# A mixture-of-experts step: spare quads moved to odd places, their up stage moved forward, selection before row broadcasts, last matrices in halves

## The chip, the cores and the metric

The kernel runs on one core of one Trainium2 chip. The metric is the device time of one execution in microseconds (us); the time before is the median of three runs. Five engines work side by side, each with its own in-order queue: TensorE (PE in the profile; its weight loads are PEld), VectorE (DVE), ScalarE (ACT), GpSimd (POOL) and SyncE (SP), which here only issues transfers (DMA) and waits. They meet at counters (semaphores): an instruction raises one when it ends, and another engine's queue stands still until the counter has reached a number.

## The reference, cut to what matters

Two layers, two streams of 128 tokens (256 tokens in all), width 1024. Each layer has a modulated norm, three mixers side by side with shared input and output projections, and then a mixture of 32 experts. The change touches only the experts:

```python
hid = silu(einsum('bnd,edf->bnef', h, moe_w1)) * einsum('bnd,edf->bnef', h, moe_w3)
return einsum('bnef,efd->bnd', hid * gate[..., None], moe_w2)
```

`gate` is not zero for two experts of one group per token, so there are 512 pairs of token and expert in a layer. Each expert has three matrices of 1 MiB in 32-bit floats: two up (1024x256) and one down (256x1024).

## The kernel before, in words

**Tiles and quads.** A tile holds up to 32 tokens of one expert; a quad is four tiles. Eight base quads hold one tile of each of the 32 experts, so their matrices are always loaded. Four spare quads hold 16 further tiles, for experts that more than 32 tokens chose. Which expert a spare tile belongs to is found at run time (`eid`, L1837 to L1840); SP reads it into a register, and the loads of a spare tile without tokens are issued under a condition that skips them. The list `ORDER` says which quad stands in which of the twelve places: before, 0, 1, 8, 2, 3, 9, 4, 5, 10, 6, 11, 7, where 8 to 11 are the spares. Two places in a row make a batch, whose 256 token slots are gathered together.

**A quad's weights.** A quad needs 12 matrices in three thirds of 4 MiB: `up_weights(i, 0)` for tiles 0 and 1 into four slots of `ring_b`, `up_weights(i, 1)` for tiles 2 and 3 into four slots of `ring`, `down_weights(i, 0)` and `(i, 1)` into the last two slots of each (L628 to L651). Each slot exists once, so a load into it waits until the product that reads it is done: the first third of place i+1 waits for the first up stage of place i (`up_psum`), the down third of place i+1 for the down stage of place i (`down_psum`). A spare quad passes through the same slots and waits, also when all its loads are skipped. SP issues, for each place i: both up thirds; then, if place i-1 was a spare, its down third; then, if i is no spare, its own down third (L665 to L675).

**A place on TensorE** (L1424 to L1451), in this order: `up(i)` if i is no spare (two stages of 64 products, for two tiles each, L1398); `gather` of a quarter of the next batch (L1380); `combine(i-1)`, which adds the result of the place before to the tokens (L1409); `gather` of another quarter; two transposes of the hidden values (L1437); if place i+1 is a spare, `up(i+1)`; then the two halves of the down product (L1449). ScalarE takes silu of the first up bank (`gated`, L948), copies every other gathered bank (L939), the transposes (L958) and the down result (`y_hi`, L963). VectorE multiplies with the gate (`hidden`, L1865), copies the other gathered banks (L1810), makes a place's combine matrix (`placed`, seven instructions, L1851 to L1856), a batch's selection matrix `S` (`select`, L1799 and L1803) and the remainder of the down result (`y_lo`, L1885).

**The front of the stage.** The hidden state is split into `h_hi` (ScalarE) and its remainder `h_lo` (VectorE, L1768), the rank of each token in its expert is a product (L1354 to L1358), VectorE works out positions (L1774 to L1789) and from them `S`. Positions and gates are also spread over all partitions as rows by two products with a matrix of ones (L1362, L1364), which `placed` needs. Then all of the first batch is gathered (32 products), four banks are zeroed (L1422), and place 0 begins. The loads of place 0 are there by then; those of place 1 start when the first up stage of place 0 is done, and wait for `eid` too (L663).

The order of all queues is written out by hand; no planner is at work.

Of the kernel before, what the change touches and what calls it, by code (L numbers as in the profile page):

```python
# [26 lines left out]
P = 128  # L27
D = 1024
# [59 lines left out]
ORDER = [0, 1, 8, 2, 3, 9, 4, 5, 10, 6, 11, 7]  # L88
# [4 lines left out]
Y_ORDER = (0, 1, 2, 3)  # L93

# [6 lines left out]
assert not any(spare(i) and spare(i + 1) for i in range(QUADS)) and not spare(0)  # L101
# [93 lines left out]
def build(nc, a, o):  # L195

    ctx = ExitStack()
    with ctx:
# [162 lines left out]
        ring_b_down_landed = sem("ring_b_down_landed")  # L361
        gf_landed = signal("gf_landed", 16)
# [132 lines left out]
        g_even = signal("g_even", 2 * BATCHES)  # L495
        g_odd = signal("g_odd", 2 * BATCHES)
# [67 lines left out]
        def _(sp):  # L564
# [11 lines left out]
            for l in range(L):  # L576
# [64 lines left out]
                def down_weights(i, p, held=None):  # L641
                    if p == 0 and i > 0:
                        sp.wait_ge(*down_psum.at(l, 2 * i))
                    for x in range(2):
# [6 lines left out]
                        sp.dma_start(into[:, 4 + x, :], src.rearrange("(p k) n -> p (k n)", k=2), **skip).then_inc(landed, 16)  # L651
# [75 lines left out]
        def _(act):  # L727
# [46 lines left out]
            for l in range(L):  # L774
# [155 lines left out]

                act.wait_ge(*rows_psum.at(l, 1))
                act.activation(posrow[:, :, :].rearrange("p a t -> p (a t)"), B[4][:, :], ACT.Copy).then_inc(rows_ready.sem, 1)
                act.wait_ge(*rows_psum.at(l, 2))
                act.activation(grow[:, :, :].rearrange("p a t -> p (a t)"), B[5][:, :], ACT.Copy).then_inc(rows_ready.sem, 1)
# [15 lines left out]
                gathered(0, 0)  # L950
                gathered(0, 2)
                for i in range(QUADS):
                    if not spare(i):
                        gated(i)
                    if i // 2 + 1 < BATCHES:
# [3 lines left out]
                    if spare(i + 1):  # L959
                        gated(i + 1)  # L960
# [20 lines left out]
        def _(pe):  # L981
# [52 lines left out]
            for l in range(L):  # L1034
# [324 lines left out]


                pe.wait_ge(*diag_ready.at(l, 1))
                pe.matmul(B[4][:, :], ones, dpos[:, :, :].rearrange("p c t -> p (c t)"), start=True, stop=True).then_inc(rows_psum.sem, 1)  # L1362
                pe.wait_ge(*diag_ready.at(l, 2))
                pe.matmul(B[5][:, :], ones, dgate[:, :, :].rearrange("p c t -> p (c t)"), start=True, stop=True).then_inc(rows_psum.sem, 1)  # L1364

                def gather(b, j):
# [3 lines left out]
                    if b == 0:  # L1370
                        if j > 1:
                            pe.wait_ge(*(g_odd if j % 2 else g_even).at(l, 1))
                    elif b > 1 or j > 0:
                        before = 2 * b + j // 2
                        pe.wait_ge(*(g_even if j % 2 else g_odd).at(l, before + j % 2))
                    bank = B[6 + j % 2] if b == 0 else B[6]
                    for k in (2 * j, 2 * j + 1):
                        for s in range(NS):
                            for h_part in (h_hi, h_lo):
                                ins = pe.matmul(bank[:, (k % 2) * BCOLS:(k % 2) * BCOLS + BCOLS], h_part[:, s, k, :], S[:, s, :],  # L1380
# [3 lines left out]
                def up(i):  # L1384

                    tokens = (xn, hT)[i // 2 % 2]
                    if i % 2 == 0:
                        pe.wait_ge(*g_even.at(l, 2 * (i // 2) + 2))
                        pe.wait_ge(*g_odd.at(l, 2 * (i // 2) + 2))
# [26 lines left out]
                for b in range(4):  # L1416
                    pe.wait_ge(*hhi_ready.at(l, b + 1))
                    pe.wait_ge(*hlo_ready.at(l, b + 1))
# [500 lines left out]
```

## Time and profile before

| | us |
|---|---|
| median of three runs (lowest, highest) | 1023.6 (1022.07, 1025.47) |
| the profiled execution's own time | 1026.62 |
| its span, first to last instruction | 1024.6 |
| TensorE busy | 781.9 (76%) |
| VectorE busy | 434.4 (42%) |
| ScalarE busy | 260.4 (25%) |
| moved by DMA | 290.51 MB, mean 284 GB/s |
| mean granted TensorE clock | 0.879 of full speed |

The profile is one execution, recorded by the hardware. Its rows give start, duration, engine, source line, what is written from what, shape and count; behind them, in brackets, how long the engine was idle before and what ended that. A window row gives the busy time of each engine in a stretch, the granted clock (1.00 is 2.4 GHz, 0.50 is 1.2 GHz) and the share and rate of the transfers. All times are counted from the start of the span. The first layer's experts run from about 215 to 536 us, the second's from about 716 to 1006 us.

### The profile page before, as it was taken

How to read it: one execution, taken by the hardware profiler on the slowest of the kernel's cores; microseconds unless marked ns; L12 is line 12 of the kernel's file. 1: busy time of each engine (PE TensorE's matmuls, PEld its weight loads, DVE VectorE, ACT ScalarE, POOL GpSimd, SP SyncE). 2: the span in 40 equal slices, each digit the busy share in tenths (PEclk: the TensorE clock that was granted, in tenths of full speed). 3: DMA queues.
4: the chain of work that ended last, by engine and by line, in shares of the span. 5: the costliest groups of instructions: out<-in, count | busy, mean ns of one | idle time of the engine just before them, and what ended most of it. 6: DMA issues, size and time to landing. Idle time of an engine off the chain costs nothing.

```text
span 1024.6 us, 17503 instructions
## 1 busy us (share of the span) xinstructions
PE 781.9 (76%) x7505; PEld 535.3 (52%) x7505; DVE 434.4 (42%) x934; ACT 260.4 (25%) x488; POOL 36.5 (4%) x52
## 2 busy tenths in 40 slices
PE   4599798977635759587967998988686759668856
PEld 3288656855323425354534984667554436445633
DVE  1357986247222214222316599843642222304214
ACT  2357226141101101101106651432320111101103
POOL 4000200000030000000000002000000000000000
PEclk9699989976868889889988998999598989979986
DMA  9945846790988697979793476529157997988681
GB/s 346 340 139 176 358 165 224 312 376 6 419 303 357 273 421 310 420 291 423 296 375 114 162 255 264 188 73 420 43 240 295 420 422 305 422 361 339 274 374 41
DMA packets 73289, 290.51 MB, mean 284 GB/s; under 512 B 8650, under 2 KB 33948, under 8 KB 47868
## 3 DMA queue, kind: packets, MB, share of 16 engines
q1 hardware_dynamic: 69174, 284.39, 70.7%
q0 software_dynamic: 1504, 3.45, 1.1%
q10 hardware_dynamic: 2534, 1.56, 0.5%
q8 instruction: 59, 0.97, 0.4%
q14 instruction: 18, 0.15, 0.0%
HBM read 382.28 MB, written 1.47 MB: 375 GB/s over the span
## 4 chain that ended last, share of the span: by engine, by line
PE 41%; DMA 32%; DVE 14%; ACT 5%; issue 4%; SPq 4%; ACTq 0%; DVEq 0%
DMA ring<-in_moe_w 24%; PE bank L1398 13%; PE bank L1064 6%; PE bank L1449 4%; DVE acc L1642 4%; PE bank L1298 4%; DMA ada<-in_ada_w 3%; PE bank L1380 3%; DMA ring<-in_ada_w 2%; SPq L639 2%; DMA ring_b<-in_moe_w 2%; PE bank L1409 2%; PE bank L1340 1%; PE bank L1007 1%; DMA ring<-in_w_in 1%
## 5 line engine op out<-in xcount | busy, mean ns | idle before, releaser
L1865 DVE SCALAR_TENSOR_TENSOR hid<-sil,gs,bank 64x256 f32<-64x256 f32 x48 | 32.5, 677 | 256.3 <-ACT sil L948 256.3
L1449 PE MATMUL bank<-ring_b,hidT 128*32 128x512 f32 x384 | 94.4, 636 | 30.3 <-issue 14.8
L1449 PE MATMUL bank<-ring,hidT 128*32 128x512 f32 x384 | 94.2, 636 | 0.0
L948 ACT ACTIVATE sil<-bank 64x256 f32<-64x256 f32 x48 | 18.2, 379 | 296.5 <-PE bank L1398 296.5
L1398 PE MATMUL bank<-ring,hT 128*32 128x256 f32 x768 | 55.3, 451 | 32.7 <-DMA ring<-in_moe_w 32.7
L1398 PE MATMUL bank<-ring,xn 128*32 128x256 f32 x768 | 53.7, 441 | 29.6 <-DMA ring<-in_moe_w 29.6
L1398 PE MATMUL bank<-ring_b,hT 128*32 128x256 f32 x768 | 51.2, 426 | 30.4 <-DMA ring_b<-in_moe_w 28.6
L1449 PEld LDWEIGHTS bank<-ring_b,hidT 128*32 128x32 f32 x384 | 24.4, 116 | 82.0 <-issue 73.1
L1885 DVE TENSOR_TENSOR y_lo<-bank,y_hi 128x512 fp32r<-128x512 f32 x48 | 32.9, 691 | 76.2 <-ACT y_hi L963 76.1
L1398 PE MATMUL bank<-ring_b,xn 128*32 128x256 f32 x768 | 48.6, 409 | 19.0 <-DMA ring_b<-in_moe_w 17.6
L1642 DVE SCALAR_TENSOR_TENSOR acc<-zp,convT,acc 128x256 f32<-128x256 f32 x120 | 61.8, 556 | 1.9
L1380 PE MATMUL bank<-S,h_hi 128*128 128x256 f32 x192 | 53.7, 312 | 10.0 <-DVE y_lo L1885 8.6
L1398 PEld LDWEIGHTS bank<-ring,hT 128*32 128x32 f32 x768 | 32.0, 130 | 55.0 <-issue 46.4
L1298 PE MATMUL bank<-mixT,ring 128*128 128x256 f32 x256 | 56.9, 381 | 2.9 <-DVE mixT L1712 1.8
L1398 PEld LDWEIGHTS bank<-ring,xn 128*32 128x32 f32 x768 | 32.4, 127 | 49.7 <-issue 40.2
L1398 PEld LDWEIGHTS bank<-ring_b,hT 128*32 128x32 f32 x768 | 28.1, 122 | 55.4 <-issue 28.9
L1064 PE MATMUL bank<-x_hi,win_hi 128*128 128x256 f32 x192 | 55.4, 289 | 2.1 <-DVE win_lo L1538 2.1
L1064 PE MATMUL bank<-x_lo,win_hi 128*128 128x256 f32 x192 | 54.3, 283 | 0.0
L1064 PE MATMUL bank<-x_hi,win_lo 128*128 128x256 f32 x192 | 54.3, 283 | 0.0
L963 ACT ACTIVATE y_hi<-bank 128x512 fp32r<-128x512 f32 x48 | 28.7, 597 | 100.4 <-PE bank L1449 100.4
L1298 PEld LDWEIGHTS bank<-mixT,ring 128*128 128x128 f32 x256 | 48.1, 190 | 10.5 <-DVE mixT L1712 2.6
L1380 PEld LDWEIGHTS bank<-S,h_hi 128*128 128x128 f32 x192 | 38.5, 201 | 22.7 <-DVE y_lo L1885 14.1
(342 smaller groups left out, 1479.6 us busy)
## 6 DMA issues: line engine op xcount, KB each, us to landing
ring_b<-in_moe_w SPq DMA_DIRECT2D x144, 1024.0 KB
ring<-in_moe_w SPq DMA_DIRECT2D x144, 1024.0 KB
ring<-in_ada_w SPq DMA_DIRECT2D x40, 1024.0 KB
ring<-in_w_in SPq DMA_DIRECT2D x14, 1024.0 KB
ada<-in_ada_w SPq DMA_DIRECT2D x4, 2048.0 KB, 23.4
ring<-in_w_out SPq DMA_DIRECT2D x8, 1024.0 KB
wuq<-in_mla_wuq POOLq DMA_DIRECT2D x2, 768.0 KB, 9.9
ring<-in_w_in SPq DMA_DIRECT2D x2, 640.0 KB
```

The lines of the kernel that those rows point to most:

```text
L639: sp.dma_start(into[:, g, :], src.rearrange("(p k) n -> p (k n)", k=KT), **skip).then_inc(landed, 16)
L948: act.activation(sil[64 * p:64 * p + 64, :], B[4 + 3 * p][64 - 64 * p:128 - 64 * p, 0:256], ACT.Silu).then_inc(sil_ready.sem, 1)
L963: act.activation(y_hi[:, 512 * half:512 * half + 512], B[5 + half][:, :], ACT.Copy).then_inc(yhi_ready.sem, 1)
L1064: ins = pe.matmul(out, weights, moving, start=(k == 0 and j == 0), stop=(k == KT - 1 and j == 2))
L1298: ins = pe.matmul(B[WOUT_BANKS[u]][:, f * T:f * T + T], w[:, k, f * P:f * P + P], mixT[:, k, :], start=(k == 4), stop=(k == 1))
L1380: ins = pe.matmul(bank[:, (k % 2) * BCOLS:(k % 2) * BCOLS + BCOLS], h_part[:, s, k, :], S[:, s, :], start=(s == 0 and h_part is h_hi), sto ...
L1398: ins = pe.matmul(B[4 + 3 * p][CAP * g:CAP * g + CAP, 0:256], tokens[:, k, c:c + CAP], w[:, g, k * 256:k * 256 + 256], start=(k == 0), sto ...
L1409: ins = pe.matmul(B[k // 2][:, (k % 2) * T:(k % 2) * T + T], y_part[:, k * P:k * P + P], ST[:, i % 2, :], start=False, stop=last, skip_gro ...
L1449: ins = pe.matmul(B[5 + half][CAP * x:CAP * x + CAP, :], hidT[:, m, CAP * x:CAP * x + CAP], w[:, 4 + x % 2, m * D + half * 512:m * D + hal ...
L1642: ins = dve.scalar_tensor_tensor(acc[:, m, :, :], src, w, acc[:, m, :, :], ALU.mult, ALU.add)
L1865: dve.scalar_tensor_tensor(hid[rows_, i % 2, :].rearrange("s (m p) -> s p m", m=2), sil[rows_, :].rearrange("s (p m) -> s p m", m=2), gs[r ...
L1885: dve.tensor_tensor(y_lo[:, 512 * half:512 * half + 512], B[5 + half][:, :], y_hi[:, 512 * half:512 * half + 512].bitcast(F32), ALU.subtra ...
```

## The change

Four edits. First, `ORDER` places every spare quad at an odd place, behind a base quad of the same batch, and both engines' loops do the spare's up stage (and `gated`, `placed`, `hidden` for it) right behind the base quad's. Second, at the front VectorE makes `S` before `h_lo` and before the row product for positions; TensorE gathers the first batch before both row broadcasts, first with `h_hi`, then with `h_lo`, into four banks that ScalarE alone copies. Third, `eid` is made later and waited for only at a spare. Fourth, the down matrices of the last place are loaded as two halves of 512 columns, all first halves ahead of all second ones, and the second half of the down product waits for the second halves alone.

In the diff, the lines of each engine stand together: SP, ScalarE, TensorE, VectorE. On VectorE, `h_lo` (L1768) and the row product for positions (L1790) move from ahead of `select(0)` to behind it, `eid` moves behind `select(1)`, and the copies of the first batch go.

```diff
-ORDER = [0, 1, 8, 2, 3, 9, 4, 5, 10, 6, 11, 7]
+ORDER = [0, 1, 2, 8, 3, 9, 4, 10, 5, 11, 6, 7]
+FIRST_PARTS = (0, 1, 3, 2)
...
-                        sp.dma_start(into[:, 4 + x, :], src.rearrange("(p k) n -> p (k n)", k=2), **skip).then_inc(landed, 16)
+                        if i < QUADS - 1:
+                            sp.dma_start(into[:, 4 + x, :], src.rearrange("(p k) n -> p (k n)", k=2), **skip).then_inc(landed, 16)
+                        else:
+                            sp.dma_start(into[:, 4 + x, :].rearrange("p (k n) -> p k n", k=2)[:, :, 0:512],
+                                         src.rearrange("(p k) n -> p k n", k=2)[:, :, 0:512]).then_inc(landed, 16)
+                def last_halves():
+                    for x in range(4):
+                        sp.dma_start((ring_b, ring)[x // 2][:, 4 + x % 2, :].rearrange("p (k n) -> p k n", k=2)[:, :, 512:D],
+                                     a["moe_w2"][l, 4 * ORDER[QUADS - 1] + x].rearrange("(p k) n -> p k n", k=2)[:, :, 512:D]).then_inc(halves_landed.sem, 16)
...
-                sp.wait_ge(*eid_ready.at(l, 1))
...
                     if spare(i):
+                        sp.wait_ge(*eid_ready.at(l, 1))
...
+                last_halves()
...
+                for i, j in enumerate(FIRST_PARTS):
+                    act.wait_ge(*g_psum.at(l, i + 1))
+                    act.activation(xn[:, 2 * j:2 * j + 2, :].rearrange("p k t -> p (k t)"), B[4 + j][:, :], ACT.Copy).then_inc(g_first.sem, 1)
...
                     if not spare(i):
                         gated(i)
+                    if spare(i + 1):
+                        gated(i + 1)
...
-                    if spare(i + 1):
-                        gated(i + 1)
...
+                def gather_first():
...
+                    for j in FIRST_PARTS[0:3]:
+                        pe.matmul(B[4 + j][:, :], zero[:, 0:P], zero[:, :], start=True, stop=False, skip_group_check=True)
+                    for b in range(4):
+                        pe.wait_ge(*hhi_ready.at(l, b + 1))
+                    pe.wait_ge(*s_ready.at(l, 1))
...
+                    for j in FIRST_PARTS[0:3]:
+                        for k in (2 * j, 2 * j + 1):
+                            part(k, h_hi)
+                    pe.wait_ge(*hlo_ready.at(l, 4))
+                    for j in FIRST_PARTS[0:3]:
+                        part(2 * j, h_lo)
+                        part(2 * j + 1, h_lo).then_inc(g_psum.sem, 1)
+                    for k in (2 * FIRST_PARTS[3], 2 * FIRST_PARTS[3] + 1):
+                        part(k, h_hi, True)
+                        ins = part(k, h_lo)
+                    ins.then_inc(g_psum.sem, 1)
...
+                gather_first()
                 for b in range(4):
                     pe.matmul(B[b][:, :], zero[:, 0:P], zero[:, :], start=True, stop=False, skip_group_check=True)
-                pe.wait_ge(*rows_ready.at(l, 2))
...
+                pe.wait_ge(*g_first.at(l, 2))
+                pe.wait_ge(*diag_ready.at(l, 1))
+                pe.matmul(B[5][:, :], ones, dpos[:, :, :].rearrange("p c t -> p (c t)"), start=True, stop=True).then_inc(rows_psum.sem, 1)
+                pe.wait_ge(*g_first.at(l, 4))
+                pe.wait_ge(*diag_ready.at(l, 2))
+                pe.matmul(B[6][:, :], ones, dgate[:, :, :].rearrange("p c t -> p (c t)"), start=True, stop=True).then_inc(rows_psum.sem, 1)
                 for i in range(QUADS):
                     if not spare(i):
                         up(i)
+                    if spare(i + 1):
+                        up(i + 1)
+                    if i == 0:
+                        pe.wait_ge(*rows_ready.at(l, 2))
...
-                    if spare(i + 1):
-                        up(i + 1)
                     pe.wait_ge(*hidT_ready.at(l, i + 1))
...
+                        if half and i == QUADS - 1:
+                            pe.wait_ge(*halves_landed.at(l, 4 * 16))
...
                     if not spare(i):
                         hidden(i)
+                    if spare(i + 1):
+                        placed(i + 1)
+                        hidden(i + 1)
                     if i // 2 + 1 < BATCHES:
                         gathered(i // 2 + 1, 2 * (i % 2) + 1)
...
-                    if i + 1 < QUADS:
+                    if i + 1 < QUADS and not spare(i + 1):
                         placed(i + 1)
-                    if spare(i + 1):
-                        hidden(i + 1)
```

## Rows read from the trace of the kernel before

**Rows 1.** Page, part 4: chain that ended last, lines, shares of the span.

```profile
DMA ring<-in_moe_w 24%; PE bank L1398 13%; PE bank L1064 6%; PE bank L1449 4%; DVE acc L1642 4%; PE bank L1298 4%; DMA ada<-in_ada_w 3%; PE bank L1380 3%; DMA ring<-in_ada_w 2%; SPq L639 2%; DMA ring_b<-in_moe_w 2%; PE bank L1409 2%; PE bank L1340 1%; PE bank L1007 1%; DMA ring<-in_w_in 1%
```

**Rows 2.** Windows, layer 1: length, busy us (instructions) by engine, clock, DMA share, GB/s.

```profile
753.50:784.00 30.50, 20.32 (x244) 12.04 (x236) 6.00 (x13) 3.91 (x8) 0.00 (x0) 0.89 0.99 411
...
791.00:852.00 61.00, 43.99 (x488) 26.55 (x481) 14.57 (x36) 8.04 (x16) 0.00 (x0) 0.89 0.99 411
852.00:858.00 6.00, 6.00 (x100) 4.00 (x102) 3.06 (x9) 0.77 (x2) 0.00 (x0) 1.00 0.08 22
...
964.50:996.00 31.50, 23.30 (x272) 12.70 (x264) 6.76 (x15) 4.29 (x9) 0.00 (x0) 0.89 0.97 396
```

**Rows 3.** Windows of layer 0, same columns.

```profile
311.00:336.50 25.50, 9.91 (x110) 6.20 (x98) 4.56 (x11) 2.55 (x5) 0.00 (x0) 0.79 0.98 408
336.50:345.50 9.00, 8.33 (x72) 3.05 (x76) 1.38 (x2) 1.20 (x2) 0.00 (x0) 0.65 0.13 16
...
385.50:391.50 6.00, 6.00 (x100) 3.99 (x103) 3.08 (x9) 0.77 (x2) 0.00 (x0) 1.00 0.06 15
```

**Rows 4.** Timeline, layer 1, PE around place 5, a spare.

```profile
843.78 5.35 PE L1398 MATMUL bank<-ring,xn 128*32 128x256 f32 x64 [4.37 <-DMA ring<-in_moe_w]
849.05 0.39 PE L1380 MATMUL bank<-S,h_hi 128*128 128x256 f32 x1
...
853.28 3.66 PE L1398 MATMUL bank<-ring_b,xn 128*32 128x256 f32 x64
...
860.21 0.60 PE L1449 MATMUL bank<-ring_b,hidT 128*32 128x512 f32 x2
...
865.27 0.39 PE L1380 MATMUL bank<-S,h_hi 128*128 128x256 f32 x1 [1.44 <-DVE y_lo L1885]
...
870.00 0.62 PE L1449 MATMUL bank<-ring_b,hidT 128*32 128x512 f32 x2 [0.47 <-ACT hidT L958]
...
873.46 3.64 PE L1398 MATMUL bank<-ring_b,hT 128*32 128x256 f32 x64
880.74 1.50 PE L1398 MATMUL bank<-ring,hT 128*32 128x256 f32 x24 [3.65 <-DMA ring<-in_moe_w]
```

**Rows 5.** Timeline, same stretch, SP's issues of transfers.

```profile
857.00 2.05 SPq L639 DMA_DIRECT2D ring_b<-in_moe_w  x4
...
863.89 0.28 SPq L651 DMA_DIRECT2D ring_b<-in_moe_w  x2
```

**Rows 6.** Timeline, same stretch, VectorE.

```profile
853.17 0.69 DVE L1810 COPY hT<-bank 128x512 f32<-128x512 f32 x1 [2.88 <-PE bank L1380]
...
857.52 0.68 DVE L1865 SCALAR_TENSOR_TENSOR hid<-sil,gs,bank 64x256 f32<-64x256 f32 x1 [1.63 <-ACT sil L948]
```

**Rows 7.** Timeline, layer 0, the front: VectorE and PE.

```profile
231.27 2.48 DVE L1768 TENSOR_TENSOR h_lo<-bank,h_hi 128x512 fp32r<-128x512 f32 x4
...
232.33 0.61 PE L1358 MATMUL bank<-both,cst 128*128 128x32 f32 x2
...
238.62 1.14 DVE L1803 SCALAR_TENSOR_TENSOR S<-row,posq,S 128x128 fp32r<-128x128 f32 x4
...
242.27 2.07 PE L1364 MATMUL bank<-dgate,cst 128*128 128x512 f32 x2 [2.59 <-DVE dgate L1833]
...
247.13 0.34 PE L1380 MATMUL bank<-S,h_hi 128*128 128x256 f32 x1
...
249.42 1.04 PE L1422 MATMUL bank<-zero 128*128 128x512 bf16 x4
...
250.56 3.66 PE L1398 MATMUL bank<-ring_b,xn 128*32 128x256 f32 x64
```

**Rows 8.** Timeline, layer 1, last down product and ScalarE's copy behind it.

```profile
999.13 1.07 PE L1449 MATMUL bank<-ring_b,hidT 128*32 128x512 f32 x2 [3.62 <-DMA ring<-in_moe_w]
...
1005.73 0.60 ACT L963 ACTIVATE y_hi<-bank 128x512 fp32r<-128x512 f32 x1 [2.31 <-PE bank L1449]
```

**Rows 9.** Window, input matrices of layer 1 arriving, columns as in rows 2.

```profile
537.00:544.00 7.00, 5.60 (x26) 3.71 (x25) 4.52 (x16) 4.28 (x6) 0.00 (x0) 1.00 1.10 349
```

More of the change, by code:

```diff
@@ L93 @@
 Y_ORDER = (0, 1, 2, 3)
+FIRST_PARTS = (0, 1, 3, 2)
 def spare(i):
     return i < QUADS and ORDER[i] >= BASE_QUADS
-assert not any(spare(i) and spare(i + 1) for i in range(QUADS)) and not spare(0)
+assert not any(spare(i) and i % 2 == 0 for i in range(QUADS))
 def ada_units(l):
@@ L361, in build @@
         ring_b_down_landed = sem("ring_b_down_landed")
+        halves_landed = signal("halves_landed", 4 * 16)
         gf_landed = signal("gf_landed", 16)
@@ L494, in build @@
         g_psum = signal("g_psum", 4 * BATCHES)
-        g_even = signal("g_even", 2 * BATCHES)
-        g_odd = signal("g_odd", 2 * BATCHES)
+        g_first = signal("g_first", 4)
+        g_even = signal("g_even", 2 * BATCHES - 2)
+        g_odd = signal("g_odd", 2 * BATCHES - 2)
         up_psum = signal("up_psum", 2 * QUADS)
@@ L1358, in _, with part @@
                 pe.matmul(B[6][:, 2 * NE:3 * NE], ones, both[:, 1, :], start=False, stop=True).then_inc(rank_psum.sem, 1)
[L1361 to L1364, printed above, removed]
+                def gather_first():
[4 more added lines that the diff above has]
+                    pe.wait_ge(*s_ready.at(l, 1))
+                    def part(k, h_part, begins=False):
+                        for s in range(NS):
+                            ins = pe.matmul(B[4 + k // 2][:, (k % 2) * BCOLS:(k % 2) * BCOLS + BCOLS], h_part[:, s, k, :], S[:, s, :],
+                                            start=(begins and s == 0), stop=(s == 1 and h_part is h_lo), skip_group_check=True)
+                        return ins
+                    for j in FIRST_PARTS[0:3]:
[9 more added lines that the diff above has]
+                    ins.then_inc(g_psum.sem, 1)
                 def gather(b, j):
@@ L1369, in gather @@
                         pe.wait_ge(*s_ready.at(l, b + 1))
[L1370 to L1376, printed above, removed]
+                    if b > 1 or j > 0:
+                        before = 4 * (b - 1) + j
+                        pe.wait_ge(*(g_even if j % 2 else g_odd).at(l, (before + 1) // 2))
                     for k in (2 * j, 2 * j + 1):
@@ L1379, in gather @@
                             for h_part in (h_hi, h_lo):
-                                ins = pe.matmul(bank[:, (k % 2) * BCOLS:(k % 2) * BCOLS + BCOLS], h_part[:, s, k, :], S[:, s, :],
+                                ins = pe.matmul(B[6][:, (k % 2) * BCOLS:(k % 2) * BCOLS + BCOLS], h_part[:, s, k, :], S[:, s, :],
                                                 start=(s == 0 and h_part is h_hi), stop=(s == 1 and h_part is h_lo))
@@ L1815, in _ @@
                 select(0)
+                for b in range(4):
+                    dve.wait_ge(*hhi_ready.at(l, b + 1))
+                    dve.tensor_tensor(h_lo[:, b // 2, :, 64 * (b % 2):64 * (b % 2) + 64], B[b][:, :].rearrange("t (p k) -> t k p", k=KT),
+                                      h_hi[:, b // 2, :, 64 * (b % 2):64 * (b % 2) + 64].bitcast(F32), ALU.subtract).then_inc(hlo_ready.sem, 1)
+                dve.tensor_tensor(dpos[:, :, :], ident.unsqueeze(1).broadcast_to([P, 2 * NS, P]),
+                                  pos[:, :, :].rearrange("p a s -> p (a s)").unsqueeze(2).broadcast_to([P, 2 * NS, P]), ALU.mult).then_inc(diag_ready.sem, 1)
                 dve.wait_ge(*rexp_ready.at(l, 2))
@@ L1834, in _ @@
                                   gts[:, :, :].rearrange("p a s -> p (a s)").unsqueeze(2).broadcast_to([P, 2 * NS, P]), ALU.mult).then_inc(diag_ready.sem, 1)
-                link(dve.tensor_tensor(past[:, :, :], ends[0:1, :].unsqueeze(1).broadcast_to([1, SPARE_TILES, NE]),
-                                       row[0:1, 0:SPARE_TILES].unsqueeze(2).broadcast_to([1, SPARE_TILES, NE]), ALU.is_le))
-                link(dve.tensor_reduce(eidf[:, :], past[:, :, :], AX_X, ALU.add))
-                dve.tensor_copy(eid[:, :], eidf[:, :]).then_inc(eid_ready.sem, 1)
-                gathered(0, 1)
-                gathered(0, 3)
                 dve.wait_ge(*rows_ready.at(l, 2))
@@ L1871, in _ @@
                 select(1)
+                link(dve.tensor_tensor(past[:, :, :], ends[0:1, :].unsqueeze(1).broadcast_to([1, SPARE_TILES, NE]),
+                                       row[0:1, 0:SPARE_TILES].unsqueeze(2).broadcast_to([1, SPARE_TILES, NE]), ALU.is_le))
+                link(dve.tensor_reduce(eidf[:, :], past[:, :, :], AX_X, ALU.add))
+                dve.tensor_copy(eid[:, :], eidf[:, :]).then_inc(eid_ready.sem, 1)
                 for i in range(QUADS):
```

29 lines of the change are left out of this document (9 added, 20 removed).

## The prediction

> **What bounds the kernel now.** I read the chain of work that ended last first. Its largest entry is the transfer of expert matrices into the ring, 24% of the span [rows 1], so I asked next, by windows, whether that transfer ever stops. In layer 1 it does. From 753.5 to 996.0 us seven base quads are loaded, 88.1 MB; two of them (25.2 MB) took the 61.0 us of the long window, 30.2 us each once its ends are taken off, 10.07 us for each third (four matrices) [rows 2]. Seven times 30.2 is 211.4, so 31.1 of the 242.5 us passed without flow: one hole at each of the four spare quads, 6.0 us in the row shown, 7 to 8.5 in the three others, 29.0 by the windows' borders. Layer 0 has three such holes (one shown; the other two are 7.0) and two of 9.0 (one shown) around the one spare quad that loads something: the stretch between those two moved 10.4 MB, 8.4 for eight up matrices and 2.0 for two spare down matrices [rows 3]. The experts' stage is thus bound by the transfer, with holes, and the question is what ends a hole.
>
> For that I read TensorE's timeline around one hole [rows 4]. I write U0, U1 for the two up stages, D for the down stage, b for a base quad and s for the spare behind it. U1(b) starts at 843.78, when its third has landed, and ends by 849.05; b's own down third is then still arriving, until about 851.8. Between 849.05 and 853.28 TensorE does 4.23 us of gathers, combine and transposes. Only then come U0(s) and U1(s), 6.93 us for both, 3.48 (half) for the first. The transfer queue issues the next base quad's first third at 857.00, when U0(s) is done [rows 5], and flow is back at about 858.6, 1.6 later. So the 4.23 us lie on the path that ends the hole; they need none of the data that is awaited.
>
> **The change, part by part. (1) Spare right behind its base quad.** The new order of TensorE is U0(b) U1(b) U0(s) U1(s), then the old work. In the first such pair of layer 1, with the clocks of [rows 4], U1(b) ends at 849.05, U0(s) 3.48 later at 852.5, flow returns at 854.1 after stopping at 851.8: a hole of 2.4 instead of 6.8.
>
> From there on places alternate base, spare, base, spare (before, mostly two bases to a spare), so the work of a pair may not fit into the 30.2 us of one base quad. From one U0(s) to the next, by [rows 4]: both spare stages 6.93; gathers, combine, transposes 4.23; the copy of the transposes, which a spare stage used to cover and now is bare, 0.47 (the idle time ahead of the second down stage); D(b) to the end of D(s) with all between, 860.21 to 873.46, 13.25; the next base's two stages, 6.93. One wait is new. VectorE now does the spare's placing and its hidden products ahead of the bank copy that D(b)'s second half waits for, and the placing waits for the combine, about 3.0 us behind U1(s). Placing takes 2.0 (853.86 to 855.89), two products 0.68 each, the copy 0.69 [rows 6]: done at 7.15. D(b)'s first half, begun at 4.70, ends at 6.43 (half of 3.44). The wait is 0.8. Bounds: 0, if the placing were done before, and 2.0 if all of it counts; I take 0.8, which comes from durations of the same instructions. Sum: 32.6 us for a pair, more than 30.2. TensorE's chain becomes the bound there, and the hole shrinks to 2.4 per pair, now split between a late down third (D(s) ends 22.2 behind U0(s), flow of the two up thirds is over at 21.7, so some 2.3) and next to nothing at the spare.
>
> Layer 1: 2.4 at the first spare, three periods of 2.4, and 2.3 for the last late down third, 12 instead of 31.1: gain 19. Layer 0: the used spare still loads behind its base quad's down third, and TensorE, now with the gathers still undone, waits for it; and its used down matrices still come behind eight up matrices, with the next down third behind them. Both holes of 9.0 stay, and I add 0.6 for the work that no longer lies in the first. The three plain holes, 20 by the windows and 21.4 with the ramps that layer 1 shows (31.1 to 29.0), become 0.3, twice 2.4 and 2.3, 7.4 in all: gain 14.0, less 0.6, 13.4. The queue of transfers gets nothing new here: the wait for the experts' numbers moves to the spare and is over long before.
>
> **(2) Selection and gather first.** In layer 0 VectorE's remainder of h (2.48 us, to 233.75) is moved behind the selection, which can then start when the rank product is there, 232.94: 0.8 at most, 0.6 with a hand-over; the row product for positions, 0.6 in the chain, goes behind it too. S is ready at 238.5 instead of 239.76, and the gather starts there, not at 244.34 behind the second row broadcast [rows 7]. Its 32 products ran 13 at 0.214 us apart and 17 at 0.128, the clock having gone from 1.2 to 2.4 GHz at 247.1, 4.8 us after the engine became steadily busy. Started cold at 238.6, about 23 run slowly: end 244.5, with the remainder (to 241.0) ready in time for the second twelve. Then four zero products 1.0 and, moved here, both row broadcasts, 2.08 each at 1.2 GHz, so 1.04 each at 2.4: U0 of quad 0 starts at 247.6 instead of 250.56. Gain 2.9 a layer, and the transfer queue, which waits for U0, starts that much earlier. Bounds: a loss of 1.0, if the clock stays low through all of it (32 times 0.214, 2.0, 4.2), and a gain of 4.8, if the engine ran at 2.4 GHz from the start (4.1, 1.0, 2.1). I take 2.9, the clock having behaved so in the row. ScalarE takes over two of VectorE's copies, 0.6 each, while the products run. The experts' numbers (1.5 us of VectorE) go behind the second selection; the hidden product of quad 0 is then late until about 254, but U1 of quad 0 lasts until then. Two layers: 5.8.
>
> **(3) Last third in halves.** D of the last quad started at 999.13 after an idle 3.62 and its second half ended by 1005.73, 6.60 at 1.2 GHz; at 2.4 GHz it takes 3.46 [rows 4, 8]. Now the first half's columns arrive 5 us earlier, so only the second half stands behind the last byte: 1.7 to 3.3 us instead of 6.6. Against that, rows of 2 KB replace rows of 8 KB. The nearest row is that of the input matrices with rows of 1 KB, 349 GB/s against 411 [rows 2, 9]; at 349 the third takes 12.0, 2.0 more. Between 0 and 2.0 I take 0.9, half-way in row size. Gain 2.6 a layer (1.3 to 4.9), 5.2 in all. The four extra issues go ahead of the next layer's input loads, which queue behind the same bytes anyhow.
>
> The Trainium skill speaks against this edit: DMA: Bandwidth & Descriptors, section Bandwidth, says to batch transfers to 1 MiB or more for at least 75% of peak, and the halves are 0.5 MiB each. At 75% of its 436 GB/s the third would take 12.8 us, an estimate from that page, and the edit would give nothing back.
>
> Sum: 19.0 + 13.4 + 5.8 + 5.2 = 43.4. The profiled execution took 1026.62 us (span 1024.6), 3.0 above the median of 1023.6; its stages carry over, so 1026.6 - 43.4 = 983.2 there, and on the median 980.2, say **980**.
>
> **Rivals.** *The pair's chain is longer than worked out.* More hand-offs between ScalarE, VectorE and TensorE than counted, or a clock that falls in them. For it: D(b)'s wait had no row of its own, and the chain is now the bound, so every microsecond counts five times (three periods in layer 1, two in layer 0). At 36 us instead of 32.6 it costs 17: 997. Against it: in [rows 4] the same steps ran through from 849 to 877 with waits of 0.47 and 1.44 only.
>
> *A skipped load is not done before the bytes queued ahead of it (slower).* A spare without tokens issues loads that are skipped, and U0(s) waits for their signal. Were it given in order, U0(s) would wait for b's down third. Place: the spare's U0. Price: it would start 2.3 behind the last byte (an estimate: 843.78 stands 2.1 behind the end of that third's flow, one third before 851.8, and 999.13 stands 3.1 behind 996.0 [rows 2, 4, 8]) and, TensorE having idled, run at 1.2 GHz, where D took 1.9 times as long; I use 6.1 instead of 3.5. Hole at the spare: 2.3 + 6.1 + 1.6 = 10.0, and the late down third 2.3 more; a pair costs 42.5 where the old holes made it 38. Layer 1 loses 18, layer 0 17, front and tail give back 11: 1048. It decides wherever the signal comes more than 5 us after the issue. Against it: the skipped down loads were issued at 863.89, after the up thirds whose second landed at 880.74, and D(s) began at 870.00 [rows 4, 5], so their signals had overtaken 10 us of data.
>
> The Trainium skill says in DMA: Bandwidth & Descriptors, section Queues, rings and completion order, that descriptors are consumed in ring order on each engine and that a signal lands only after all earlier writes; by that rule the rival is what happens. The rows disagree, at least for skipped loads.
>
> *The hole is not ended by U0(s).* If something else held the queue, only front and tail stay: about 1013. Against it is the issue at 857.00 within 0.25 us of U0(s)'s end. *The halves cost what they save:* 349 GB/s or worse leaves 983 to 986.
>
> **How the numbers follow.** The forecast has 0.73 (its own range 968 to 992: the new wait between 0 and 2.0 over five pairs is minus 4 to plus 6, the front plus 8 to minus 4, the tail plus or minus 4 or so, hardly all at one end), the longer chain 0.12, the halves 0.06, the wrong releaser 0.04, the skipped loads 0.05. The range 966 to 1002 holds the first three. A measurement of this kernel tells about 0.3%, 3 us, from no change: faster 0.92, same 0.03, slower 0.05.
>
> **What would show it.** After the change the windows of layer 1 should show holes of about 2 to 3 us; U0(s) right behind U1(b) with no wait on a transfer; D(b)'s second half waiting under 1 us; a pair in 32 to 33 us with TensorE busy throughout at 2.4 GHz; layer 0's two long holes unchanged; U0 of quad 0 3 us closer to the rank product; only one half of D behind the last byte. I am wrong if holes over 5 us remain at the plain spares, or if U0(s) waits for a transfer there.

## The result, and the profile after

The changed kernel takes 984.76 us (median of four runs, 983.79 to 985.76), the kernel before 1022.84 in the same set: a ratio of 0.9624, 95% interval 0.9602 to 0.9646, 38.1 us less. The forecast was 980, with 966 to 1002 as its range. The two profiled executions, 1026.62 and 983.79 us, differ by 42.8: the one of before was 3.0 longer than the median of 1023.6, the one of after is the shortest of its set.

The page's chain that ended last has changed hands:

```profile
PE 49%; DMA 22%; DVE 17%; ACT 5%; SPq 3%; issue 3%; ACTq 0%; DVEq 0%
PE bank L1432 15%; DMA ring<-in_moe_w 9%; PE bank L1490 6%; PE bank L1080 6%; DMA ring_b<-in_moe_w 6%; PE bank L1314 4%; DVE acc L1683 4%; PE bank L1443 3%; DMA ada<-in_ada_w 3%; PE bank L1412 3%; DMA ring<-in_ada_w 2%; PE bank L1023 2%; SPq L643 2%; PE bank L1356 1%; PE bank L1386 1%
```

The transfer into `ring` fell from 24% [rows 1] to 9%, that into `ring_b` rose from 2% to 6%; the up products, the down product, combine and gather together make 27%. (Lines moved: up products L1432, gather L1412, combine L1443, transposes L1478, down product L1490, first zero products L1452, row broadcasts L1457 and L1460.)

**The pairs.** The windows of layer 1 around its first two pairs, then of layer 0 (columns as in rows 2):

```profile
793.00:798.00 5.00, 5.00 (x100) 3.14 (x96) 0.01 (x1) 0.38 (x1) 0.00 (x0) 1.00 0.47 141
798.00:816.50 18.50, 15.37 (x140) 9.86 (x136) 8.28 (x23) 3.88 (x8) 0.00 (x0) 1.00 1.01 424
816.50:820.00 3.50, 3.50 (x60) 1.70 (x54) 2.78 (x8) 0.84 (x2) 0.00 (x0) 1.00 0.39 96
820.00:829.50 9.50, 9.50 (x182) 5.72 (x178) 1.38 (x2) 1.14 (x3) 0.00 (x0) 1.00 1.00 417
829.50:831.00 1.50, 1.50 (x33) 0.90 (x29) 0.00 (x0) 0.00 (x0) 0.00 (x0) 1.00 0.94 322
...
330.00:339.00 9.00, 7.62 (x104) 3.92 (x108) 0.00 (x0) 0.38 (x1) 0.00 (x0) 0.69 0.10 22
364.00:373.50 9.50, 7.83 (x80) 3.04 (x84) 1.38 (x2) 1.19 (x2) 0.00 (x0) 0.70 0.13 25
403.00:406.00 3.00, 3.00 (x52) 1.54 (x48) 2.62 (x8) 0.68 (x2) 0.00 (x0) 1.00 0.33 90
```

I count a hole as its length times the share of the flow that is missing. The hole at a plain spare of layer 1 that [rows 2] show, the second of that layer, was 5.7 us (6.00 times 1 - 22/411). Now the hole at the first spare is 3.3 (5.0 times 1 - 141/424) and the one at the next spare 0.3. Each pair has a new hole instead: the next base quad's down third starts late, since it waits for D(s). That is 2.7 in layer 1 (window from 816.5) and 2.4 in layer 0 (window from 403.0), where the plain hole of [rows 3] was 5.8. Layer 0's two long holes are as they were, 8.5 and 8.9 (the one in [rows 3] was 8.7).

TensorE through the first pair, from U1(b) to the next pair's U1(s) (timeline, layer 1):

```profile
786.95 4.89 PE L1432 MATMUL bank<-ring,hT 128*32 128x256 f32 x64 [3.51 <-DMA ring<-in_moe_w]
791.65 3.64 PE L1432 MATMUL bank<-ring_b,hT 128*32 128x256 f32 x64
795.11 3.64 PE L1432 MATMUL bank<-ring,hT 128*32 128x256 f32 x64
803.40 0.62 PE L1490 MATMUL bank<-ring_b,hidT 128*32 128x512 f32 x2 [0.47 <-ACT hidT L976]
806.07 0.62 PE L1490 MATMUL bank<-ring_b,hidT 128*32 128x512 f32 x2 [0.74 <-DVE xn L1842]
809.43 0.39 PE L1412 MATMUL bank<-S,h_hi 128*128 128x256 f32 x1 [1.44 <-DVE y_lo L1926]
814.16 0.62 PE L1490 MATMUL bank<-ring_b,hidT 128*32 128x512 f32 x2 [0.47 <-ACT hidT L976]
817.62 3.64 PE L1432 MATMUL bank<-ring_b,xn 128*32 128x256 f32 x64
821.07 3.64 PE L1432 MATMUL bank<-ring,xn 128*32 128x256 f32 x64
824.52 3.64 PE L1432 MATMUL bank<-ring_b,xn 128*32 128x256 f32 x64
827.98 3.64 PE L1432 MATMUL bank<-ring,xn 128*32 128x256 f32 x64
```

U1(b) itself still waited 3.51 for its third. U0(s) stands right behind it at 791.65 and waits for nothing. From there to the next U0(s) at 824.52 are 32.87 us, the four up stages at the end without a wait. No wait in these 32.87 us is for a transfer; all are hand-overs of ScalarE or VectorE. The granted clock is 1.00 (2.4 GHz) in every window of layer 1 shown above. VectorE's part, and SP's issues:

```profile
801.84 0.35 DVE L1884 TENSOR_SCALAR ST<-posrow,cst 128x256 f32<-128x256 f32 x1 [8.83 <-PE bank L1443]
...
803.88 1.41 DVE L1898 SCALAR_TENSOR_TENSOR hid<-sil,gs,bank 64x256 f32<-64x256 f32 x2
805.32 0.69 DVE L1842 COPY xn<-bank 128x512 f32<-128x512 f32 x1
```

```profile
783.93 0.99 SPq L643 DMA_DIRECT2D ring_b<-in_moe_w  x4
...
795.35 2.45 SPq L643 DMA_DIRECT2D ring_b<-in_moe_w  x4
798.81 1.77 SPq L643 DMA_DIRECT2D ring<-in_moe_w  x4
808.05 0.28 SPq L657 DMA_DIRECT2D ring_b<-in_moe_w  x2
808.42 0.24 SPq L657 DMA_DIRECT2D ring<-in_moe_w  x2
...
828.22 2.06 SPq L643 DMA_DIRECT2D ring_b<-in_moe_w  x4
```

The placing waits for the combine until 801.84, the hidden products follow, and the bank copy ends at 806.0: the 0.74 ahead of D(b)'s second half. The issue at 783.93 is the spare's first up third, skipped; those at 795.35 and 798.81 are the next base quad's up thirds. The base quads' issues are 32.87 us apart (795.35, 828.22), later ones 32.91 and 32.87.

**The front** of layer 0 (TensorE, then VectorE), with S, the gather and the broadcasts in their new order:

```profile
232.09 0.61 PE L1374 MATMUL bank<-both,cst 128*128 128x32 f32 x2
...
244.53 1.04 PE L1452 MATMUL bank<-zero 128*128 128x512 bf16 x4
245.40 1.02 PE L1457 MATMUL bank<-dpos,cst 128*128 128x512 f32 x2
246.26 1.02 PE L1460 MATMUL bank<-dgate,cst 128*128 128x512 f32 x2
247.21 3.66 PE L1432 MATMUL bank<-ring_b,xn 128*32 128x256 f32 x64
```

```profile
237.19 1.14 DVE L1835 SCALAR_TENSOR_TENSOR S<-row,posq,S 128x128 fp32r<-128x128 f32 x4
238.25 2.48 DVE L1852 TENSOR_TENSOR h_lo<-bank,h_hi 128x512 fp32r<-128x512 f32 x4
```

From the last rank product to U0 of quad 0 are 15.12 us, where [rows 7] have 18.23; in layer 1, 15.65 for 18.37.

**The tail**: layer 1's last place, then the windows in which the last up third and, behind it, both halves arrive.

```profile
950.43 5.07 PE L1432 MATMUL bank<-ring,hT 128*32 128x256 f32 x64 [5.13 <-DMA ring<-in_moe_w]
958.31 0.62 PE L1490 MATMUL bank<-ring_b,hidT 128*32 128x512 f32 x2 [0.47 <-ACT hidT L976]
960.99 0.62 PE L1490 MATMUL bank<-ring_b,hidT 128*32 128x512 f32 x2 [0.76 <-DMA ring<-in_moe_w]
```

```profile
935.00:947.00 12.00, 6.98 (x76) 2.57 (x68) 1.87 (x3) 0.98 (x2) 0.00 (x0) 0.80 1.01 420
947.00:957.00 10.00, 6.57 (x77) 4.22 (x78) 0.68 (x1) 0.38 (x1) 0.00 (x0) 0.83 1.04 388
```

One half of D lies behind the last byte here; in layer 0 none does, D starting at 513.11 and running through without a wait for a transfer. The first update of the tokens (`xT`) follows at 964.22 and, in layer 0, at 518.06.

Whole stages, in the two profiled executions:

| us | before | after |
|---|---|---|
| layer 0, first up issue of place 1 to first `xT` | 254.32 to 536.59: 282.3 | 250.93 to 518.06: 267.1 |
| layer 1, the same | 752.38 to 1006.97: 254.6 | 731.55 to 964.22: 232.7 |

That is 15.2 and 21.9, and with the front's 3.1 and 2.7 it makes 42.9 of the 42.8 by which the two executions differ.

### The profile page after: what moved, and what is told of

Its sections match the earlier page's. It is cut to its first block, busy times and chain, and to the rows that moved or that the text cites. A ratio compares the mean times of both kernels' runs of the same rounds, so it can differ in the third digit from the quotient of the medians.

```text
span 981.8 us, 17517 instructions
## 1 busy us (share of the span) xinstructions
PE 772.8 (79%) x7509; PEld 521.5 (53%) x7511; DVE 431.3 (44%) x930; ACT 262.6 (27%) x492; POOL 36.4 (4%) x52
## 3 DMA queue, kind: packets, MB, share of 16 engines
q0 software_dynamic: 1504, 3.45, 1.0%
## 4 chain that ended last, share of the span: by engine, by line
PE 49%; DMA 22%; DVE 17%; ACT 5%; SPq 3%; issue 3%; ACTq 0%; DVEq 0%
PE bank L1432 15%; DMA ring<-in_moe_w 9%; PE bank L1490 6%; PE bank L1080 6%; DMA ring_b<-in_moe_w 6%; PE bank L1314 4%; DVE acc L1683 4%; PE bank L1443 3%; DMA ada<-in_ada_w 3%; PE bank L1412 3%; DMA ring<-in_ada_w 2%; PE bank L1023 2%; SPq L643 2%; PE bank L1356 1%; PE bank L1386 1%
## 5 line engine op out<-in xcount | busy, mean ns | idle before, releaser
L1490 PE MATMUL bank<-ring_b,hidT 128*32 128x512 f32 x384 | 96.3, 639 | 36.7 <-DMA ring<-in_moe_w 11.3
L1898 DVE SCALAR_TENSOR_TENSOR hid<-sil,gs,bank 64x256 f32<-64x256 f32 x48 | 32.6, 679 | 160.1 <-ACT sil L966 159.6
L1490 PE MATMUL bank<-ring,hidT 128*32 128x512 f32 x384 | 96.2, 639 | 0.0
L1432 PE MATMUL bank<-ring_b,hT 128*32 128x256 f32 x768 | 55.0, 450 | 40.4 <-DMA ring_b<-in_moe_w 40.4
L1490 PEld LDWEIGHTS bank<-ring_b,hidT 128*32 128x32 f32 x384 | 21.4, 116 | 93.4 <-issue 62.8
L1432 PEld LDWEIGHTS bank<-ring_b,hT 128*32 128x32 f32 x768 | 28.8, 129 | 69.1 <-issue 34.9
L1432 PE MATMUL bank<-ring,hT 128*32 128x256 f32 x768 | 50.8, 424 | 18.0 <-DMA ring<-in_moe_w 18.0
L1926 DVE TENSOR_TENSOR y_lo<-bank,y_hi 128x512 fp32r<-128x512 f32 x48 | 32.6, 690 | 64.3 <-ACT y_hi L979 63.6
L1432 PE MATMUL bank<-ring,xn 128*32 128x256 f32 x768 | 46.5, 397 | 8.5 <-DMA ring<-in_moe_w 8.5
L1432 PE MATMUL bank<-ring_b,xn 128*32 128x256 f32 x768 | 48.0, 406 | 6.5 <-DMA ring_b<-in_moe_w 6.5
L1412 PE MATMUL bank<-S,h_hi 128*128 128x256 f32 x160 | 41.5, 294 | 12.9 <-DVE y_lo L1926 11.5
L1884 DVE TENSOR_SCALAR ST<-posrow,cst 128x256 f32<-128x256 f32 x24 | 8.5, 355 | 98.2 <-PE bank L1443 89.2
L1432 PEld LDWEIGHTS bank<-ring,hT 128*32 128x32 f32 x768 | 27.8, 122 | 39.5 <-issue 26.6
L1443 PE MATMUL bank<-ST,y_hi 128*128 128x256 f32 x192 | 47.9, 287 | 0.6 <-DVE y_lo L1926 0.6
```

The costliest lines, as they stand in the source:

```text
L1412: ins = pe.matmul(B[6][:, (k % 2) * BCOLS:(k % 2) * BCOLS + BCOLS], h_part[:, s, k, :], S[:, s, :], start=(s == 0 and h_part is h_hi), sto ...
L1432: ins = pe.matmul(B[4 + 3 * p][CAP * g:CAP * g + CAP, 0:256], tokens[:, k, c:c + CAP], w[:, g, k * 256:k * 256 + 256], start=(k == 0), sto ...
L1443: ins = pe.matmul(B[k // 2][:, (k % 2) * T:(k % 2) * T + T], y_part[:, k * P:k * P + P], ST[:, i % 2, :], start=False, stop=last, skip_gro ...
L1490: ins = pe.matmul(B[5 + half][CAP * x:CAP * x + CAP, :], hidT[:, m, CAP * x:CAP * x + CAP], w[:, 4 + x % 2, m * D + half * 512:m * D + hal ...
L1898: dve.scalar_tensor_tensor(hid[rows_, i % 2, :].rearrange("s (m p) -> s p m", m=2), sil[rows_, :].rearrange("s (p m) -> s p m", m=2), gs[r ...
L1926: dve.tensor_tensor(y_lo[:, 512 * half:512 * half + 512], B[5 + half][:, :], y_hi[:, 512 * half:512 * half + 512].bitcast(F32), ALU.subtra ...
```

## The experiments

**1. Each part alone.** Four kernels, each the kernel before with a part of the change, compared with it in one set (its median there 1024.16). The order alone, one line:

```diff
-ORDER = [0, 1, 8, 2, 3, 9, 4, 5, 10, 6, 11, 7]
+ORDER = [0, 1, 2, 8, 3, 9, 4, 10, 5, 11, 6, 7]
```

> The kernel before with only the new order of places; the spare's up stage stays behind the gathers, combine and transposes. Theory (the hole at a plain spare is ended by U0(s), which waits for 4.2 us of other work): the holes stay near 7 us each, a pair takes about 37 us (22 from U0(s) until the next base quad's loads are through, 7 of hole, the rest waiting for the third), and the time is 1014 to 1024, against 1022.8 before. Rival (the order itself is what pays, since spares now share a batch with the base quad before them): 990 to 1000, as in the full change less front and tail.

Measured 1013.75, ratio 0.9903 (0.9870 to 0.9936), 10.4 us less, just under the range of the theory. Its layer 1, TensorE and SP in one pair:

```profile
828.83 0.62 PE L1449 MATMUL bank<-ring_b,hidT 128*32 128x512 f32 x2 [0.47 <-ACT hidT L958]
832.28 3.64 PE L1398 MATMUL bank<-ring_b,xn 128*32 128x256 f32 x64
839.64 6.20 PE L1398 MATMUL bank<-ring,xn 128*32 128x256 f32 x64 [3.72 <-DMA ring<-in_moe_w]
849.94 3.66 PE L1398 MATMUL bank<-ring_b,xn 128*32 128x256 f32 x64
```

```profile
815.83 2.22 SPq L639 DMA_DIRECT2D ring_b<-in_moe_w  x4
...
853.66 2.01 SPq L639 DMA_DIRECT2D ring_b<-in_moe_w  x4
```

A pair takes 37.8 us (815.83 to 853.66; the two others 35.3 and 37.0). U1(b) ends at about 845.8, and U0(s) starts 4.1 later, at 849.94, behind the gathers, as in [rows 4]. Added up over windows of half a microsecond, its holes at the plain spares are 3.8 to 7.8 us, where the kernel before has 6.8 to 8.6. Where the rest of the 10.4 comes from was not taken apart.

The order and the spare's stage moved forward (all of part 1, and nothing else). The order is as above; this is TensorE's part, cut. ScalarE's `gated` and VectorE's `placed` and `hidden` move with it.

```diff
                     if not spare(i):
                         up(i)
+                    if spare(i + 1):
+                        up(i + 1)
...
-                    if spare(i + 1):
-                        up(i + 1)
```

> The kernel before with the new order and the spare's up stage right behind the base quad's; front and last third as before. Theory: a pair takes 32.9 us as in the full change, holes of 2 to 4 us in place of 7, and the time is 30 us less than before, 991 to 996. Rival (front and tail carry more of the gain than the 11 us that I gave them): 1003 or more.

Measured 993.24, ratio 0.9702 (0.9667 to 0.9737), 30.9 us less. The pairs of layer 1 take 32.87, 32.83 and 32.87. So the move is worth 20.5 of part 1, the order 10.4.

The front alone (the second and third edits of the change; TensorE's part, cut):

```diff
+                gather_first()
                 for b in range(4):
                     pe.matmul(B[b][:, :], zero[:, 0:P], zero[:, :], start=True, stop=False, skip_group_check=True)
-                pe.wait_ge(*rows_ready.at(l, 2))
```

> The kernel before with selection and gather ahead of the row broadcasts alone; old order, old place of the spare's up stage, whole last third. Theory: the first up stage starts 2.9 to 3.2 us earlier in each layer and nothing else moves: 1016 to 1018, against 1022.8. Rival (the transfers that restart earlier meet something else, or the hidden product that is now late holds up place 0): 1020 to 1024.

Measured 1019.75, ratio 0.9950 (0.9927 to 0.9972): 4.4 us less by the medians, 2.9 to 7.5 by the interval. The median lies between the two ranges expected. The halves alone (cut):

```diff
+                last_halves()
...
+                        if half and i == QUADS - 1:
+                            pe.wait_ge(*halves_landed.at(l, 4 * 16))
```

> The kernel before with the last place's down matrices in halves alone. Theory: one half of the last down product no longer stands behind the last byte, less about 0.9 us for rows of 2 KB: 1 to 4 us in each layer, 1016 to 1020. Rival (the halves arrive as slowly as a page's rule for transfers under 1 MiB says, 12.8 us for the third): 1022 to 1024.

Measured 1020.91, ratio 0.9970 (0.9951 to 0.9989): 3.2 us less, 1.1 to 5.0, again between the two ranges. The three parts add up to 38.5, the whole to 38.1; the parts do not depend on each other within what can be told.

**2. Is TensorE's chain the bound now?** Three kernels made from the changed one, in one set with it again (before: 1023.96).

> The changed kernel again, as the base for the runs beside it: 983 to 987 us, whatever the theory.

Measured 985.17 (983.45 to 985.89). First, a longer chain:

```diff
+                    if spare(i):
+                        for b in range(5):
+                            pe.matmul(B[4][:, :], zero[:, 0:P], zero[:, :], start=True, stop=True, skip_group_check=True)
```

> The changed kernel with five products with zeros, 128x512, put on TensorE behind each spare's down stage, about 1.1 us at 2.4 GHz. Theory, TensorE's chain bounds the pairs: a pair takes 34.0 instead of 32.9, and the five or six pairs that bound in two layers add 5 to 7: 990 to 992. Rival, the transfers bound: 984 to 986, since the ballast would lie beside a transfer.

Measured 990.14 (984.45 to 991.21), 5.0 more. The windows from one pair's first issue to the next, of the changed kernel and then of this one:

```profile
797.75:830.62 32.87, 29.79 (x396) 18.22 (x392) 12.42 (x32) 5.87 (x12) 0.00 (x0) 1.00 0.92 368
830.62:863.48 32.86, 29.76 (x396) 18.14 (x392) 12.40 (x32) 5.87 (x12) 0.00 (x0) 1.00 0.95 385
```

```profile
798.30:832.51 34.21, 30.96 (x400) 18.84 (x397) 12.43 (x32) 5.86 (x12) 0.00 (x0) 1.00 0.92 368
832.51:866.72 34.21, 30.94 (x400) 18.47 (x397) 12.43 (x32) 5.86 (x12) 0.00 (x0) 1.00 0.92 370
```

These pairs are longer by 1.34, the third of layer 1 by 1.30. TensorE's busy time grew by 1.18, with four of the five products of each pair in the records (32 of 40 in the whole run) and 0.16 of idle time where the fifth would stand. None of it was hidden: the transfers are not the bound of these pairs. Over all spares of both layers the spans from issue to issue grew by 9.8, and the kernel by 5.0 only: the last places of both layers, behind the pairs, took 1.1 and 1.5 less than in the profile of the changed kernel beside it, and layer 1's places ahead of its first pair 2.4 less. So the pairs are bound by TensorE's chain, and a part of what they lose is made up elsewhere. Then a shorter chain. VectorE copies the bank for D(b)'s second half before it places the spare:

```diff
-                    if spare(i + 1):
-                        placed(i + 1)
-                        hidden(i + 1)
                     if i // 2 + 1 < BATCHES:
                         gathered(i // 2 + 1, 2 * (i % 2) + 1)
...
+                    if spare(i + 1):
+                        placed(i + 1)
+                        hidden(i + 1)
```

> VectorE copies the gathered bank ahead of the spare's placing and hidden products, not behind them. Theory, TensorE's chain bounds the pairs: the 0.74 us that D(b)'s second half waited for that copy leave the chain, a pair takes 32.1 instead of 32.9, and with some seven such places in two layers the kernel gains about 5: 979 to 981. But placing and hidden products then end some 0.7 later; if the spare's transposes are held up by that instead, the wait only moves and nothing is gained. Rival, the transfers bound the pairs: 984 to 986, periods as before.

Measured 979.44 (976.99 to 981.14), 5.7 less than the changed kernel, ratio to the kernel before 0.9571 (0.9552 to 0.9589). The 0.74 is gone and the spare's transposes are not held up. One row of its timeline in layer 1 is new:

```profile
848.14 3.66 PE L1432 MATMUL bank<-ring,hT 128*32 128x256 f32 x64 [0.25 <-DMA ring<-in_moe_w]
```

Its pairs take 32.0, 32.4 and 32.3, not 32.1 throughout, since U1(b) now waits 0.25, and 0.19 in the pair after, for its own transfer. That is a second loop, only just shorter than TensorE's chain: issue behind U0(s), two thirds of flow, U1(b), U0(s), issue. In the pair of this row the issue is at 822.92, U1(b) starts 25.22 later, U0(s) 3.45 behind it, and the next issue follows after 3.72: 32.39. Last, on top of that, the combine in two parts, so that its first half stands where TensorE waited 1.44 for `y_lo` (cut):

```diff
+                    if i > 0:
+                        combine(i - 1, 0)
...
-                        combine(i - 1)
+                        combine(i - 1, 1)
```

> As copy_first, and the combine (sum of a place's result into the tokens) is split in two, its first four products ahead of the gather, so that they fill the 1.44 us for which the gather ahead of D(s) waited for VectorE's remainder of the down result. Theory, TensorE's chain bounds: a pair takes 31.0 to 31.5, still above the 30.2 of the transfers, and the kernel takes 974 to 978. Rival, transfers bound: no change from 984 to 986. Third way: the first products wait for the same remainder themselves, then it is as copy_first.

Measured 974.30 (970.89 to 976.82), ratio 0.9520 (0.9496 to 0.9545). The time came out as expected, but not the pairs:

```profile
788.78:820.53 31.75, 29.75 (x396) 19.10 (x391) 12.45 (x32) 5.87 (x12) 0.00 (x0) 1.00 0.95 384
820.53:851.70 31.17, 29.57 (x396) 18.61 (x392) 12.42 (x32) 5.87 (x12) 0.00 (x0) 1.00 0.98 392
851.70:885.53 33.83, 29.76 (x394) 19.07 (x390) 12.41 (x32) 5.87 (x12) 0.00 (x0) 1.00 0.98 396
```

```profile
878.37 3.66 PE L1432 MATMUL bank<-ring,xn 128*32 128x256 f32 x64 [2.48 <-DMA ring<-in_moe_w]
```

One pair reaches 31.17, the next waits 2.48 in front of U1(b) for its transfer; the mean of the three, 32.25, is that of copy_first. Of the 1.44, 0.65 is left, now in front of the first half of the combine. So both kernels ran once more in one set (before: 1023.27).

> The kernel of copy_first again: 978 to 981 if its median holds, pairs of layer 1 in 32.0 to 32.4 us with the base's U1 waiting a little for its transfer.

> The kernel of copy_combine again. Theory, a shorter TensorE chain lets one or two pairs run in 31.2, and then the transfers make up for it with a wait in front of U1(b), so the mean of the pairs is that of copy_first, 32.2, in both layers, and the kernel is worth little over copy_first: 977 to 980, the 974 having been a lucky set. Rival, the products ahead of the gather shorten other places too (bases that wait for nothing): 972 to 976 again, with layer 0's stretch from its first issue to the first update of the tokens 2 to 3 us shorter than copy_first's, as in the two profiles.

Measured 977.99 (974.27 to 980.76) and 975.87 (974.46 to 977.33). The second lies within the rival's 972 to 976 and misses the theory's 977 to 980. But what the rival went by is not there: layer 0's stretch, 3.0 shorter with the split in the first two profiles, is 264.7 and 264.3 here. The pairs of layer 1 take 32.1 and 31.9 in the mean. The medians of ten runs of each are 978.4 and 975.3: splitting the combine is worth some 3 us, and where they lie is not settled. It is the best version of this study, 47 to 50 us below the kernel before.

**3. What the halves are worth within the change.** The changed kernel with whole matrices in the last place, the halves' lines of the diff taken back:

```diff
-                last_halves()
...
-                        if half and i == QUADS - 1:
-                            pe.wait_ge(*halves_landed.at(l, 4 * 16))
```

> The changed kernel with the last place's down matrices loaded whole again. Over the runs so far the stretch from the start of the last place's U1 to the first update of the tokens took 13.8 to 14.2 us in each layer with halves, and 14.7 to 19.2, mean 16.2, without. Theory, the halves save about 2.2 a layer, since the down product can in no case start before U1's own chain is done: the stretch is 14.7 to 16.5 in both layers, its down product waits 1 to 3 for a transfer, and the kernel takes 988 to 990. The prediction's price, 2.6 a layer: 990 or a little over. Rival, with halves the product of layer 0 found everything landed, so they are worth something in layer 1 alone: 987, and layer 0's stretch stays near 14.

Measured 986.04 (981.56 to 986.76), ratio 0.9625 (0.9590 to 0.9660), which is the ratio of the changed kernel, 0.9624. The last place of layer 0 in it:

```profile
504.20 6.36 PE L1422 MATMUL bank<-ring,hT 128*32 128x256 f32 x64 [3.84 <-DMA ring<-in_moe_w]
514.13 0.62 PE L1478 MATMUL bank<-ring_b,hidT 128*32 128x512 f32 x2 [1.25 <-DMA ring<-in_moe_w]
```

The stretches are 14.9 and 16.4 us, the waits 1.25 and 2.21, as expected. The changed kernel's two profiles have 14.2 and 13.8 in layer 0 and 13.8 twice in layer 1, so whole matrices cost 0.6 to 1.0 and 2.6 there, and yet the median is only 0.9 to 1.3 above those of the changed kernel, which come from other sets. Here the theory's 988 to 990 missed, and the rival's 987 is nearer, though its reason (a stretch near 14 in layer 0) is not quite what the row shows. Where the rest went stays open; the interval allows for 3 us either way.

## Why the prediction was right, and where its sizes were off

**The bound and what ends a hole** were right. The move of U0(s) alone, on top of the order, took 20.5 us, and in the order-only kernel the holes stayed, ended by a U0(s) behind the gathers. The rival in which something else held the queue falls with that.

**Part 1, the pair's chain.** Predicted 32.6 us for a pair, measured 32.87; the new wait of D(b)'s second half was predicted as 0.8, measured as 0.74, and its removal gave 5.7 us. That TensorE's chain would become the bound of the pairs is shown from both sides, by the longer and by the shorter chain. The gain was predicted as 32.4 and measured as 30.9 (26.9 to 34.1) alone. In layer 1 the first hole was mis-sized, 3.3 instead of 2.4: the step let U1(b) follow 2.1 us behind the end of its third's flow, as its row did. Here it followed by 3.7 (the third behind it stopped flowing at about 793.3, so U1's own at 783.2, 10.07 earlier; U1 starts at 786.95), and ran 4.89 where the row had 5.35. Added up over windows of half a microsecond, layer 1 has 14.0 of holes from its first pair on, where 12 were forecast. Layer 0 kept its two long holes, and its plain ones add up to 7.4, as priced. What the prediction did not name is the second loop through U1(b)'s own transfer; as far as these runs go it holds the pairs near 32 in the mean (31.9 to 32.3 in the four profiles with a shorter chain), though one reached 31.17.

**Part 2, the front**, came out by its steps: S ready at 238.3 (predicted 238.5), the gather over at 244.5 (244.5), U0 at 247.21 (247.6), 3.1 and 2.7 a layer for the 2.9 predicted. The 4.4 of the kernel with the front alone does not contradict the 5.8.

**Part 3, the halves, is the term that was mis-sized**: 5.2 predicted, 3.2 measured alone, about 1 within the change and there not clear of noise. Two things failed in it. The price of the old tail came from one row, layer 1's D at 1.2 GHz after an idle 3.62 [rows 8]: in that execution U1 of the last place to `xT` took 19.2 us, and 14.7 to 16.8 in the seven other layers recorded without halves before this step was tested (the order, the pairs and the front alone, and layer 0 of the kernel before). And D has a second predecessor that the step did not look at: its own hidden values. With halves D's first product follows its transposes by 0.47, with no transfer to wait for, and `xT` comes 13.7 to 14.3 us behind U1's start in every layer recorded with halves. Earlier bytes could have helped D's second half alone, which waits for a transfer in eight of these sixteen layers, by 0.4 to 0.8 us (0.76 in the row shown). The rows of 2 KB cost what was put down for them: 388 GB/s against 420, 0.8 us on ten (0.9 predicted). The rule of the Trainium skill (DMA: Bandwidth & Descriptors, section Bandwidth) that asks for 1 MiB for 75% of peak did not decide here: eight transfers of 0.5 MiB in a row ran at 388 GB/s, 89% of the page's 436.

**The sum and the median.** The sum, 43.4, is within 0.6 of what the two profiled executions show, and in part that is luck: from place 1 to the start of the last U1 they differ by 12.6 and 16.5 us in the two layers, 29.1 where part 1 had 32.4, and from there to `xT` by 2.6 and 5.4, 7.9 where part 3 had 5.2. On the medians the sum is 5 too large. The halves' term is 2 of that; the others lie within the intervals of the single parts. The step from the profile to the median carried the sum over whole. That part of it, such as the tail of [rows 8], came from what made that execution 3 us longer than the median is likely, but one profile of the kernel before does not show it.

**The slower rival**, skipped loads that signal behind queued data, falls with the pair's timeline. At the place that it named, U0(s) begins at 791.65, behind the skipped up loads issued at 783.93, while the base quad's down third, queued ahead of them, flows until about 793.3. Then the issues at 808.05 and 808.42 are the spare's skipped down loads, the next base's up thirds issued from 795.35 flow until 816.5, and D(s) at 814.16 waits 0.47 for its transposes and for no transfer. So the rule of the Trainium skill (DMA: Bandwidth & Descriptors, section Queues, rings and completion order), by which a signal lands only after every earlier write of its DMA engine, did not hold back the signal of a skipped load here.

## What to carry to other kernels

When a transfer ring stands still, look for the consumer that frees the next slot and for work ahead of it that needs none of the awaited data; moving the consumer forward is worth at most that work, once per hole (here 20.5 us, of 4.2 at each of seven plain spares). Then work out the consumer engine's whole chain per period, hand-overs of the helping engines included, because it takes over as the bound, and single waits of 0.7 us in it become the next thing to remove. Price a tail from more than one row of its kind, and look at both predecessors of its last product.

## What the hardware showed that was not expected

- The signals of skipped loads overtake data: a transfer that its condition skips, issued at 808.42, had raised its signal by 814.16, when D(s) began, though data issued before it flowed until 816.5.
- Cutting a matrix into two transfers with rows of 2 KB cost little flow: 388 GB/s against 420 in the window ahead of it with rows of 8 KB, 8% less, where the input matrices with rows of 1 KB had 349 [rows 9].
